# Two fp32r products in place of each f32 attention value product, split and rearranged, in a fused hybrid attention kernel

## The reference, cut to what matters

```python
logits = einsum('bthd,btjhd->bthj', q_b, k_g) * Dh ** -0.5   # keys: chosen by top-k, and by chunk
p = softmax(where(valid, logits, -inf))
o_a = einsum('bthj,btjhd->bthd', p, v_g)
y_a = (o_a * silu(a_z)) @ w_branch_a
h_b = head_norm(sigmoid(b_o) * cell, head_norm_g)
y_b = (h_b * silu(b_z)) @ w_branch_b
merged = sigmoid(g_a) * y_a + sigmoid(g_b) * y_b
out = rmsnorm(x + merged @ w_out, final_norm_g)
```

## Time and profile before

| | |
|---|---|
| median of 3 runs | 515.21 us (515.03 to 515.23) |
| the profiled execution | 515.22 us |
| its span, first to last instruction | 513.5 us |
| TensorE busy | 503.4 us (98%), 2506 matmul records |
| VectorE, ScalarE, GpSimd busy | 252.1, 236.3, 214.0 us |
| mean granted clock | 0.999 of full |

### The profile page before, as it was taken

One profiled execution on the slowest core, in us unless ns is written; L12 is line 12 of the kernel. 1 busy time (PEld: TensorE's weight loads), 2 busy tenths in 40 slices (PEclk: granted clock), 3 DMA queues, 4 the chain that ended last, 5 costly groups with the idle time before them and its releaser, 6 DMA issues.

```text
span 513.5 us, 6778 instructions
## 1 busy us (share of the span) xinstructions
PE 503.4 (98%) x2506; PEld 422.1 (82%) x2506; DVE 252.1 (49%) x564; ACT 236.3 (46%) x417; POOL 214.0 (42%) x142
## 2 busy tenths in 40 slices
PE   7999999999999999999999999999999999999995
PEld 7688888888888878788888888888888888887885
DVE  3875778877999915515645556311110011125333
ACT  6756754655534344455567643233321333152322
POOL 1675231333353442356486343056335653372000
PEclk9999999999999999999999999999999999999999
DMA  8744531222233422122213111142244426443112
GB/s 281 207 132 121 142 99 47 83 83 70 63 114 87 139 83 82 42 60 66 82 41 84 42 43 41 42 123 66 60 122 123 110 57 202 124 155 133 41 48 77
DMA packets 44841, 48.94 MB, mean 95 GB/s; under 512 B 4996, under 2 KB 29700, under 8 KB 44808
## 3 DMA queue, kind: packets, MB, share of 16 engines
q1 hardware_dynamic: 43944, 47.39, 31.4%
q10 hardware_dynamic: 864, 1.12, 0.6%
HBM read 46.40 MB, written 2.11 MB: 94 GB/s over the span
## 4 chain that ended last, share of the span: by engine, by line
PE 91%; DMA 3%; POOL 3%; issue 1%; ACT 1%; SPq 1%; DVE 0%; POOLq 0%; DVEq 0%; ACTq 0%
PE pj L1397 23%; PE pj L1398 22%; PE pj L1399 22%; PE ob L1504 3%; DMA w_raw<-in_w_in 2%; POOL w_lo L510 2%; PE tr L1498 2%; PE ob L1478 2%; PE qb L1468 2%; PE qb L1463 2%; PE qb L1462 2%; PE ob L1398 1%; PE qb L1398 1%; PE qb L1397 1%; PE ob L1397 1%; PE ob L1399 1%
## 5 line engine op out<-in xcount | busy, mean ns | idle before, releaser
L510 POOL TENSOR_TENSOR w_lo<-w_raw,w_hi 128x1024 fp32r<-128x1024 f32 x70 | 168.3, 2415 | 147.1 <-ACT w_hi L851 147.0
L1397 PE MATMUL pj<-w_hi,h_hi 128*128 128x512 f32 x272 | 112.8, 415 | 0.0
L1399 PE MATMUL pj<-w_hi,h_lo 128*128 128x512 f32 x272 | 106.5, 392 | 0.0
L1398 PE MATMUL pj<-w_lo,h_hi 128*128 128x512 f32 x272 | 106.5, 392 | 0.0
L1397 PE MATMUL pj<-h_hi,w_hi 128*128 128x512 f32 (+1 forms) x200 | 78.1, 390 | 1.0 <-DVE h_lo L1076 1.0
L851 ACT ACTIVATE w_hi<-w_raw 128x1024 fp32r<-128x1024 f32 (+1 forms) x72 | 73.5, 1045 | 9.6 <-DMA w_raw<-in_w_out 6.0
L1399 PE MATMUL pj<-h_hi,w_lo 128*128 128x512 f32 (+1 forms) x200 | 77.9, 389 | 0.0
L1398 PE MATMUL pj<-h_lo,w_hi 128*128 128x512 f32 (+1 forms) x200 | 77.9, 389 | 0.0
L1399 PEld LDWEIGHTS pj<-w_hi,h_lo 128*128 128x128 f32 x272 | 51.1, 188 | 11.4
L1397 PEld LDWEIGHTS pj<-w_hi,h_hi 128*128 128x128 f32 x272 | 51.2, 188 | 9.5 <-issue 1.0
L1398 PEld LDWEIGHTS pj<-w_lo,h_hi 128*128 128x128 f32 x272 | 51.3, 189 | 9.3 <-issue 1.0
(11 more groups left out here) (200 smaller groups left out, 828.8 us busy)
## 6 DMA issues: line engine op xcount, KB each, us to landing
w_raw<-in_w_in SPq DMA_DIRECT2D x60, 512.0 KB, 3.6
w_raw<-in_w_out SPq DMA_DIRECT2D x5, 512.0 KB, 3.6
x_tok<-in_x SPq DMA_DIRECT2D x4, 512.0 KB, 5.4
w_raw<-in_w_branch_a SPq DMA_DIRECT2D x8, 256.0 KB, 2.9
w_raw<-in_w_branch_b SPq DMA_DIRECT2D x8, 256.0 KB, 3.3
x_again<-in_x SPq DMA_DIRECT2D x1, 2048.0 KB, 9.0
w_late<-in_w_out SPq DMA_DIRECT2D x3, 512.0 KB, 7.2
neg_m_all<-neg_m_d SPq DMA_DIRECT2D x4, 256.0 KB, 5.0
```

Source lines behind the costliest of these rows:

```text
L510: eng.tensor_tensor(lo[:, 0:m], raw_slot(n)[:, 0:m], hi[:, 0:m].bitcast(F32), ALU.subtract).then_inc(lo_by_dve if n in DVE_SLOTS else lo_b ...
L1397: pe.matmul(bank, a_hi, b_hi, start=first, stop=False)
L1398: pe.matmul(bank, a_hi, b_lo, start=False, stop=False)
L1399: return pe.matmul(bank, a_lo, b_hi, start=False, stop=last)
```

## The change

1. The probabilities are split: ScalarE copies the transposed block, rounded, from the bank to `probs_hi`, and VectorE writes the remainder `probs_lo`. On VectorE this job now comes last in its place, behind the logits.
2. The values are split once into `v_pair` (each head's rounded 64 columns beside its 64 remainder columns). GpSimd makes the rounded half at place 4 (`V_SPLIT`), in two casts; VectorE subtracts at place 6, in two instructions.
3. `pv_a` is two fp32r matmuls for each key block: `probs_hi` with both halves of the values, 128 columns, and `probs_lo` with the rounded half, 64 columns. Four heads fill a bank instead of eight, so VectorE finishes every four heads: reciprocal, a copy of one half, an addition of the other, and a multiplication.
4. GpSimd writes the second branch's gated product into `cell`, where it is transposed from; the four jobs `out_b_chan` move to places 43 to 46. The ring `gated` is free for the next unit once GpSimd has read it.
5. The first two output units run over seven of their eight slots first, one after the other, and then over the eighth.
6. VectorE scales 640 columns at the end and ScalarE 384.

```diff
@@ -107,6 +107,9 @@
+V_SPLIT = first_quarter("bo") + 4
...
@@ -145,7 +148,7 @@
     for j in range(TILES):
-        put(first["bz"] + 4 * j + 7, "out_b_chan", j)
+        put(attn_place(len(ATTN) + 4 + j), "out_b_chan", j)
         if j < TILES - 1:
...
@@ -156,6 +159,7 @@
     [(TILES - 1, 1, slice(WIDTH, WIDTH + WIDTH // 2)), (TILES - 1, 2, slice(WIDTH + WIDTH // 2, 2 * WIDTH))]
+SHARE = 640
 LAST_SIDE = ("out_a_chan", TILES - 1)
...
@@ -172,7 +176,7 @@
         ring = RING_OF[job[0]]
-        if job[0] == "pv_a" and ATTN[job[1]][1]:
+        if job[0] == "pv_a" and ATTN[job[1]][1] % 4:
             bank[job] = bank[("pv_a", job[1] - 1)]
...
@@ -330,11 +334,13 @@
         v_a = at("v_a", [P, TILES, WIDTH], F32, z_d)
+        v_pair = at("v_pair", [P, TILES, A_HEADS, 2, A_DIM], F32R, z_a)
+        probs_lo = at("probs_lo", [P, 2, SEQ], F32R, z_d)
         stage = at("stage", [P, 2, WIDTH], F32, z_h)
         conv_acc = at("conv_acc", [P, 2, SEQ], F32, z_h)
         probs = at("probs", [P, 2, SEQ], F32, z_h)
-        probs_t = at("probs_t", [P, 2, SEQ], F32, z_h + 4096)
+        probs_hi = at("probs_hi", [P, 2, SEQ], F32R, z_h + 4096)
         gated = at("gated", [P, 2, WIDTH], F32, z_h + 8192)
...
@@ -544,9 +553,10 @@
             elif kind == "probs_chan":
-                eng.wait_ge(probs_t_made, job[1] + 1)
+                eng.wait_ge(probs_lo_made, job[1] + 1)
             elif kind == "pv_a":
-                eng.wait_ge(o_a_made, ATTN[job[1]][0] + 1)
+                i, h = ATTN[job[1]]
+                eng.wait_ge(o_a_made, 2 * i + h // 4 + 1)
             else:
...
@@ -732,6 +742,13 @@
                         pool.wait_ge(q_lo_zeroed, e + 1)
+                if p == V_SPLIT:
+                    wait_full(pool, ("pv_b", B_HEADS - 1, TILES - 1))
+                    for j in range(0, TILES, 2):
+                        pool.tensor_copy(v_pair[:, j:j + 2, :, 0, :],
+                                         v_a[:, j:j + 2, :].rearrange("p t (h d) -> p t h d", d=A_DIM))\
+                            .then_inc(v_hi_made, 1)
                 if p in SPLIT_AT:
...
@@ -778,7 +795,8 @@
                 pool.wait_ge(b_normed, j + 1)
-                pool.tensor_tensor(ring, ring, cell[:, j, :, 0:B_DIM], ALU.mult).then_inc(gated_b_made, 1)
+                c = cell[:, j, :, 0:B_DIM]
+                pool.tensor_tensor(c, ring, c, ALU.mult).then_inc(gated_b_made, 1)
...
@@ -918,6 +936,13 @@
                         .then_inc(probs_made, 1)
+                elif kind == "probs_chan":
+                    s = job[1]
+                    w = (ATTN[s][0] + 1) * P
+                    wait_full(act, job)
+                    if s >= 2:
+                        wait_full(act, ("pv_a", s - 2))
+                    act.activation(probs_hi[:, s % 2, 0:w], bank_of(job)[:, 0:w], ACT.Copy).then_inc(probs_hi_made, 1)
                 elif kind in ("out_a_chan", "out_b_chan"):
...
@@ -1047,10 +1072,10 @@
                     act.wait_ge(y_gained, m + 1)
-                    half = y_norm[:, i % 2, WIDTH:D_MODEL]
+                    half = y_norm[:, i % 2, SHARE:D_MODEL]
                     act.activation(half, half, ACT.Copy, scale=out_rstd[:, i:i + 1]).then_inc(y_scaled_act, 1)
                     act.wait_ge(y_scaled_act, i + 1)
-                    act.dma_start(out.rearrange("(t p) d -> p t d", p=P)[:, i, WIDTH:D_MODEL], half)\
+                    act.dma_start(out.rearrange("(t p) d -> p t d", p=P)[:, i, SHARE:D_MODEL], half)\
                         .then_inc(stored[i % 2], 16)
...
@@ -1236,22 +1261,25 @@
                     w = (ATTN[s][0] + 1) * P
-                    wait_full(dve, job)
-                    if s >= 2:
-                        wait_full(dve, ("pv_a", s - 2))
-                    dve.tensor_copy(probs_t[:, s % 2, 0:w], bank_of(job)[:, 0:w]).then_inc(probs_t_made, 1)
+                    dve.wait_ge(probs_hi_made, s + 1)
+                    if s == 0:
+                        dve.wait_ge(v_lo_made, 2)
+                    dve.tensor_tensor(probs_lo[:, s % 2, 0:w], bank_of(job)[:, 0:w],
+                                      probs_hi[:, s % 2, 0:w].bitcast(F32), ALU.subtract).then_inc(probs_lo_made, 1)
                 elif kind == "pv_a":
                     s = job[1]
                     i, h = ATTN[s]
-                    if h == A_HEADS - 1:
+                    if h % 4 == 3:
                         wait_full(dve, job)
                         dve.wait_ge(probs_made, s + 1)
-                        rec = p_rec[:, s - h:s + 1]
-                        link(dve.reciprocal(rec, p_sum[:, s - h:s + 1]))
-                        dve.tensor_tensor(o_a[:, i, :].rearrange("p (h d) -> p h d", d=A_DIM),
-                                          bank_of(job)[:, :].rearrange("p (h d) -> p h d", d=A_DIM),
-                                          rec.unsqueeze(2).to_broadcast([P, A_HEADS, A_DIM]), ALU.mult)\
+                        rec = p_rec[:, s - 3:s + 1]
+                        half = o_a[:, i, (h - 3) * A_DIM:(h + 1) * A_DIM].rearrange("p (h d) -> p h d", d=A_DIM)
+                        both = bank_of(job)[:, :].rearrange("p (h a d) -> p h a d", a=2, d=A_DIM)
+                        dve.reciprocal(rec, p_sum[:, s - 3:s + 1])
+                        link(dve.tensor_copy(half, both[:, :, 0, :]))
+                        link(dve.tensor_tensor(half, both[:, :, 1, :], half, ALU.add))
+                        dve.tensor_tensor(half, half, rec.unsqueeze(2).to_broadcast([P, 4, A_DIM]), ALU.mult)\
                             .then_inc(o_a_made, 1)
...
@@ -1262,6 +1290,14 @@
+            def split_values():
+                for n, j in enumerate(range(0, TILES, 2)):
+                    dve.wait_ge(v_hi_made, n + 1)
+                    dve.tensor_tensor(v_pair[:, j:j + 2, :, 1, :],
+                                      v_a[:, j:j + 2, :].rearrange("p t (h d) -> p t h d", d=A_DIM),
+                                      v_pair[:, j:j + 2, :, 0, :].bitcast(F32), ALU.subtract).then_inc(v_lo_made, 1)
...
@@ -1299,8 +1335,10 @@
                     dve.wait_ge(gate_t_made, n + 1)
-                    if m >= 2:
-                        wait_full(dve, OUT_ORDER[m - 2])
+                    if 2 <= m < 2 + TILES:
+                        dve.wait_ge(gated_b_made, m - 1)
+                    elif m >= 2 + TILES:
+                        wait_full(dve, ("out_a_chan", m - 2 - TILES))
                     ring = gated[:, m % 2, :]
...
@@ -1326,7 +1364,9 @@
                     p = 4 * u + q
-                    for job in SIDE.get(p, []):
+                    if p == V_SPLIT + 2:
+                        split_values()
+                    for job in sorted(SIDE.get(p, []), key=lambda job: job[0] == "probs_chan"):
                         job_side(job)
...
@@ -1385,7 +1425,7 @@
                     dve.wait_ge(y_gained, m + 1)
-                    dve.tensor_scalar(y_norm[:, i % 2, 0:WIDTH], y_norm[:, i % 2, 0:WIDTH], out_rstd[:, i:i + 1], None,
+                    dve.tensor_scalar(y_norm[:, i % 2, 0:SHARE], y_norm[:, i % 2, 0:SHARE], out_rstd[:, i:i + 1], None,
                                       ALU.mult).then_inc(y_scaled, 1)
...
@@ -1500,14 +1540,20 @@
                     wait_read(pe, ("probs_chan", s))
+                    c = h % 4 * 2 * A_DIM
                     for j in range(i + 1):
-                        ins = pe.matmul(bank[:, h * A_DIM:(h + 1) * A_DIM], probs_t[:, s % 2, j * P:(j + 1) * P],
-                                        v_a[:, j, h * A_DIM:(h + 1) * A_DIM], start=(j == 0), stop=(j == i))
+                        hi, lo = probs_hi[:, s % 2, j * P:(j + 1) * P], probs_lo[:, s % 2, j * P:(j + 1) * P]
+                        if j == i > 0:
+                            pe.matmul(bank[:, c:c + A_DIM], lo, v_pair[:, j, h, 0, :], start=False, stop=False)
+                            ins = pe.matmul(bank[:, c:c + 2 * A_DIM], hi, v_pair[:, j, h, :, :], start=False, stop=True)
+                        else:
+                            pe.matmul(bank[:, c:c + 2 * A_DIM], hi, v_pair[:, j, h, :, :], start=(j == 0), stop=False)
+                            ins = pe.matmul(bank[:, c:c + A_DIM], lo, v_pair[:, j, h, 0, :], start=False, stop=(j == i))
                 elif kind in ("out_a_chan", "out_b_chan"):
                     pe.wait_ge(gated_a_made if kind == "out_a_chan" else gated_b_made, job[1] + 1)
-                    ring = gated[:, OUT_ORDER.index(job) % 2, :]
                     for b in range(KW):
-                        ins = pe.transpose(bank[:, b * P:(b + 1) * P], ring[:, b * P:(b + 1) * P], ident[:, :])
+                        src = gated[:, job[1] % 2, b * P:(b + 1) * P] if kind == "out_a_chan" else cell[:, job[1], b, 0:B_DIM]
+                        ins = pe.transpose(bank[:, b * P:(b + 1) * P], src, ident[:, :])
                 ins.then_inc(side_done, 1)
...
@@ -1569,17 +1615,27 @@
-            for m, (i, piece, cols) in enumerate(OUT_UNITS):
```

(16 more changed lines are left out.)

## The result

The changed kernel took **520.5 us** (median of four runs, 518.9 to 520.5) against 515.2 us before: a ratio of 1.0097, with a 95% interval of 1.0084 to 1.0109. It is slower by 5.3 us where 3.8 were forecast; 519.0 was the forecast time and 520.5 the upper end of its range. The profiled execution has a span of 518.8 us, 513.5 before. The first row is the busy time of the page, which answers the earlier trace rows; the second is the window of the earlier trace rows (engines PE, PEld, DVE, ACT, POOL, then granted clock, DMA share and GB/s).

A forecast was written before the change was run, and what follows sets the result against it. TensorE, busy 503.4 us of a 513.5 us span, was taken to bound the kernel. 515.2 + 4.9 (attention waits) - 1.0 (interleaved output units) - 0.1 (last scaling) = 519.0 us; range 516.0 to 520.5.

The forecast's parts named there:

- value product on TensorE: Attention's 160 value matmuls: two weight loads per pair before and after, 0.112 us each, so 0 (-9 to +5 us).
- (a): Before the first value product: casting and subtracting the values delays first logits and query split; +1.9 us.
- (b): Place 14: the separate multiplication of four heads' output waits for GpSimd's remainder, delaying TensorE at place 16; +0.5 us.
- (c): Place 19: second query split runs late behind a late exponential and two rounded copies, delaying the value product; +0.9 us.
- (d): Place 22: the multiplication of four heads' output again waits for GpSimd's remainder, delaying TensorE's next matmul; +0.3 us.
- (e): Place 27: third query split runs late behind late logits, three rounded copies and the normalisation; +1.1 to 1.3 us.
- records under 0.09: Sign that the forecast is wrong: value-product records on TensorE less than 0.09 us apart, where 0.11 was expected.
- no exclusion at all: Rival, chance 0.08: GpSimd's casts and remainders do not hold VectorE back; split costs 1.0 us, time 515.1 us, no change.
- faster: Rival, chance 0.08: values split in time, or value product cheaper, and only the end counts; 514.1 us.
- the ledger: Place-by-place timing of the attention stage from row durations and queue orders; gave the waits summing to 4.9 us.
- the copies cost more: Rival, chance 0.10: ScalarE's rounded copies take 0.1 us more each and casts 1.3; 520.3 to 521 us.
- only the value split costs: Rival, chance 0.19: the small multiplication slips between GpSimd's remainders, later attention waits shrink to 0.1; 516.1, up to 517.6 us.

The follow-up runs named there:

- the run with that one edit: Changed kernel with VectorE subtracting the rounded probabilities before, not behind, the remainder of the transposed branch output at places having both: 519.2 us.

## Why the prediction was right and wrong

The terms, measured against the kernel with everything but the split, in the traces:

| step | forecast | measured |
|---|---|---|
| value product on TensorE | 0 (-9 to +5) | +0.8 |
| (a) splitting the values | +1.9 | +1.6 |
| (b) multiplication at place 14 | +0.5 | +0.3 |
| (c) second query split, place 19 | +0.9 | +0.8 |
| (d) multiplication at place 22 | +0.3 | +0.45 |
| (e) third query split, place 27 | +1.1 to 1.3 | +1.15 |
| place 39 | no wait | **+1.4** |
| moved transposes | 0 (at worst +0.3) | 0 (at most +0.03; -0.1 by the medians) |
| interleaved output units | -1.0 | -0.95 by the traces, -1.3 by the medians |
| last scaling | -0.1 (0 to -0.3) | +0.05 by the traces, +0.16 by the medians |

From its first query-key product to its last instruction the changed kernel takes 5.5 us more than the one before, 280.9 against 275.4; the measured column adds up to that within 0.1.

**Right:** the sign and, in the main, the mechanism of the five waits that were named. TensorE has no slack in this stage, the f32 product bought nothing by being split, and the price is the chain behind it. The five waits sum to 4.3 us against 4.9 forecast, each at its place. The value product was taken at 0 "because inside a run of short matmuls each load is exposed"; doubling it gave 0.112 and 0.109 us a matmul, the number of the rows. Both ends of its range, taken from single rows of 0.06 and 0.14, are refuted, and so is the sign "records under 0.09" for being wrong: single starts are 0.06 and 0.08 apart here, and the group cost what was forecast. Refuted is also the estimate from the 81 ns that the Trainium skill, "TensorE: Matmul & The Clock Gate", section "Back-to-back issue gap", gives for 128 columns: these runs give 109 to 112 ns for 64 columns already, and 0.22 us for a product of 128 columns and one of 64 together.

**Right, and stronger than put:** the exclusion. The trace had one case at 512 columns; these have 256 and 1024, three times 2.0 to 2.7 us for 0.42, and the reading from a bank ended it. The Trainium skill, "SBUF — State Buffer", section "Who interferes with whom", says that a VectorE instruction with two SBUF inputs contends with a GpSimd instruction that reads SBUF, and that the order of issue decides who blocks; the rows at 253.21, 271.16 and 293.11 agree, each ending 0.3 us behind the remainder. So the rival *no exclusion at all* is refuted, and *faster* with it: the first logits came at 240.60 and not before 239.6.

**Wrong, the step that failed:** "Behind it, tiles 2 and 3 have places of 2.7 to 3.1 us and no split: no wait in the ledger." The ledger followed the chain of the probabilities place by place, and gave each of its banks two places. It left out that the branch outputs' transposes draw from the same ring of two banks. At place 38 they shorten that to one place, and there the change's new order on VectorE puts the subtraction last. The order was in the diff (the `sorted` line), and I used it only to place the logits ahead. Without this term the changed kernel takes 519.2 us, as the run with that one edit shows, 0.2 from the forecast. That closeness is partly luck, since the product's 0.8 us and the waits, 0.6 smaller than forecast, offset each other. So is 520.5 falling in the rival *the copies cost more* (520.3 to 521): the casts took 1.04 us and the rounded copies 0.26 at 128 columns, no more than was put in.

**Wrong in size:** the value product by 0.8 us, spread over 32 heads; (a) and (b) were 0.5 too large together. In (a) the first logits stood where I had put them; behind them the second logits followed after 1.54 us instead of 1.67, and the rounded copy began 0.1 us before the query split's record ended. TensorE's idle time ahead of the first value product, named as a sign with 1.5 to 2.3 us, was 1.2 by the brackets, though that product came 1.6 late.

**Right number, wrong reason:** (c) and (e) were put down to the late multiplications and to the added rounded copies together ("late by (b) and by two rounded copies", "three rounded copies and the normalisation"). With the multiplication out of the lock both went to nothing, the rounded copies still there. They use up slack but did not reach TensorE there. So the first rival, "only the value split costs", had the right structure: with (b) cured, (b) to (e) vanish.

The kernel with that cure gave 517.8 us; less the 1.4 of place 39 and the 0.8 of the product it would be 515.6. The rival's 516.1 is near that, though without the product's 0.8, which no case had.

**Not settled:** why each head's value product costs 0.02 to 0.03 us more than the f32 form, although its pairs inside the group cost the same. What differs is the 128 columns of the hi product and which of the two ends the group, and no run parts these. That the two levels of the changed kernel's times are the race at 271.15 us is argued from three kernels and not shown in one.

## What to carry to other kernels

When an engine in the middle of a chain gets one more instruction, count for each ring of buffers who else takes from it, and in which order the reader frees them: two places of slack can be one where a second user comes in. Before splitting a small f32 product in rounded parts, look at how many weight loads it takes, since they and not the streamed columns may be its price; here the split kept their number, and at its best cost 0.9 us. And if a short VectorE instruction sits beside long GpSimd ones, give it an input from a bank: one operand changed took 2.7 us off, more than any reordering did.

## What the runs showed of the hardware

- The exclusion works both ways, in turns: two VectorE subtractions (1.22 us each alone) and two GpSimd ones (2.62 together alone) that met took 4.38 and 4.48 us. At 271 us VectorE's multiplication came 7 ns behind a remainder and took 2.67 us; where it came 0.09 us ahead of one, it took 0.42, and GpSimd's remainder 2.58 and 2.59 us, not 2.39.
- A tensor that is added up in its bank and multiplied from there costs VectorE the same 0.42 us at 256 columns as one from SBUF, with no lock.
- One more fp32r matmul of 64 columns and one more record of an f32 product of 64 columns cost nearly the same, 0.109 and 0.112 us. In a group that alternates, the fp32r matmul of 128 columns is followed after 0.14 us and that of 64 after 0.08, 0.22 for both, the price of two f32 records.
